# Two transformer blocks on one core: the gate columns ride on the attention's value stage, ahead of the query tiles

## What is computed

```python
hN = _rmsnorm(x, norm_g[l])
p = _split_in(hN @ w_in[l])          # m_q m_k m_v m_o m_z | m_i m_f | n_q n_kc n_vc n_ks n_vs n_kw n_vw | n_g ...
mh = _mlstm(silu(conv(p["m_q"])), silu(conv(p["m_k"])), p["m_v"],
            p["m_i"] + b_igate[l], p["m_f"] + b_fgate[l])
gates = jax.nn.sigmoid(p["n_g"] + b_nsa_gate[l])
# in _mlstm, per head: log_f = log_sigmoid(f_pre); a = cumsum(log_f)
# m_t = running maximum of (log_i - a) plus a; the decays are exp(... - m_t)
```

## Time and profile before

| what | value |
|---|---|
| median of 3 runs | 1860.36 us |
| the profiled execution's own time | 1859.45 us |
| its span | 1857.5 us |
| TensorE busy | 1838.0 us (99%) |
| VectorE busy | 1036.8 us (56%) |
| ScalarE busy | 738.3 us (40%) |
| chain that ended last | TensorE 91%, VectorE 5% |
| mean DMA rate | 118 GB/s |

### The profile page before, as it was taken

How to read it: one execution, slowest core, us unless ns; L and a number is a source line. 1 busy time by engine, 2 the same in 40 slices (tenths; PEclk the granted TensorE clock), 3 DMA queues, 4 the chain that set the end, 5 groups by cost and what they waited for, 6 DMA issues and landing times.

```text
span 1857.5 us, 25669 instructions
## 1 busy us (share of the span) xinstructions
PE 1838.0 (99%) x9436; PEld 1524.5 (82%) x9436; DVE 1036.8 (56%) x1511; ACT 738.3 (40%) x1312; POOL 219.6 (12%) x278
## 2 busy tenths in 40 slices
PE   8999999999999999999999999999999999999998
PEld 6888878777888888888889888888888888888887
DVE  7888756765576653333435797556334763333332
ACT  5345444565333542322224763335222442222332
POOL 1101041000010400000011155053000100000010
PEclk9999999999999999999999999999999999999999
DMA  8867823211476333333334433313334333332331
GB/s 312 301 177 214 227 80 92 68 37 50 131 242 206 96 91 90 102 93 94 95 93 122 140 96 95 87 29 86 102 96 152 91 91 96 96 102 88 107 94 52
DMA packets 352230, 218.86 MB, mean 118 GB/s; under 512 B 41981, under 2 KB 336202, under 8 KB 351502
## 3 DMA queue, kind: packets, MB, share of 16 engines
q1 hardware_dynamic: 340022, 173.22, 32.9%
q0 software_dynamic: 11504, 40.79, 6.6%
q10 hardware_dynamic: 616, 3.67, 0.5%
HBM read 208.83 MB, written 9.99 MB: 118 GB/s over the span
## 4 chain that ended last, share of the span: by engine, by line
PE 91%; DVE 5%; issue 2%; ACT 1%; DMA 1%; DVEq 0%; ACTq 0%; SPq 0%; POOLq 0%
PE psum L443 27%; PE psum L445 26%; PE psum L444 26%; PE psum L1674 2%; DVE ada_sum L2503 1%; DVE mlstm_qk_T L2503 1%; PE psum L1472 1%; PE psum L1502 1%; PE psum L1379 1%; PE psum L1363 1%; PE psum L1483 1%; DMA ada_w<-in_ada_w 1%; PE psum L1567 0%; DVE delta_qkv_T L2503 0%; DVE act_lo L2503 0%
## 5 line engine op out<-in xcount | busy, mean ns | idle before, releaser
L443 PE MATMUL psum<-act_hi,w_hi 128*128 128x512 f32 (+1 forms) x1632 | 651.0, 399 | 3.1 <-DVE w_lo L402 1.2
L445 PE MATMUL psum<-act_hi,w_lo 128*128 128x512 f32 (+1 forms) x1632 | 633.5, 388 | 0.0
L444 PE MATMUL psum<-act_lo,w_hi 128*128 128x512 f32 (+1 forms) x1632 | 632.9, 388 | 0.0
L402 DVE TENSOR_TENSOR w_lo<-w_raw,w_hi 128x1024 fp32r<-128x1024 f32 x304 | 382.1, 1260 | 293.5 <-ACT w_hi L394 270.9
L394 ACT ACTIVATE w_hi<-w_raw 128x1024 fp32r<-128x1024 f32 x304 | 317.6, 1052 | 179.8 <-PE psum L445 166.5
L443 PEld LDWEIGHTS psum<-act_hi,w_hi 128*128 128x128 f32 x1632 | 306.9, 188 | 69.1 <-issue 6.1
L445 PEld LDWEIGHTS psum<-act_hi,w_lo 128*128 128x128 f32 x1632 | 306.7, 188 | 64.2
L444 PEld LDWEIGHTS psum<-act_lo,w_hi 128*128 128x128 f32 x1632 | 307.2, 188 | 59.7 <-issue 1.4
L443 PE MATMUL psum<-ffn_hi,w_hi 128*128 128x512 f32 (+1 forms) x396 | 145.8, 368 | 0.0
L445 PE MATMUL psum<-ffn_hi,w_lo 128*128 128x512 f32 (+1 forms) x396 | 144.8, 366 | 0.0
L444 PE MATMUL psum<-ffn_lo,w_hi 128*128 128x512 f32 (+1 forms) x396 | 144.8, 366 | 0.0
(11 more groups left out here) (409 smaller groups left out, 2280.5 us busy)
## 6 DMA issues: line engine op xcount, KB each, us to landing
w_raw<-in_ffn_w_in SPq DMA_DIRECT2D x88, 512.0 KB, 3.7
w_raw<-in_w_in SPq DMA_DIRECT2D x68, 512.0 KB, 3.8
w_raw<-in_mix_w_in SPq DMA_DIRECT2D x52, 512.0 KB, 3.7
ada_w<-in_ada_w POOLq DMA_DIRECT2D x48, 512.0 KB, 4.9
w_raw<-in_ffn_w_out SPq DMA_DIRECT2D x32, 512.0 KB, 3.8
late_ada_w<-in_ada_w POOLq DMA_DIRECT2D x24, 512.0 KB, 4.8
w_raw<-in_ffn_w_out SPq DMA_DIRECT2D x16, 384.0 KB, 3.3
w_raw<-in_w_branch_a SPq DMA_DIRECT2D x8, 512.0 KB, 4.7
```

The lines of the kernel that those rows point to most:

```text
L402: dve.tensor_tensor(WLO[:, n % 4, :], RAW[:, n % 4, :], WHI[:, n % 4, :].bitcast(F32), ALU.subtract).then_inc(w_lo, 1)
L443: pe.matmul(out, whi, hhi, start=start, stop=False)
L444: pe.matmul(out, whi, hlo, start=False, stop=False)
L445: return pe.matmul(out, wlo, hhi, start=False, stop=stop)
```

## The change

The stage `small1` goes. `vsw1` moves ahead of `nsa1` and its rows become 288 columns wide: 256 of values, then 24 and 8 gate columns. Its weights come in three chunks of 3, 3 and 2 row blocks rather than two of four. The token groups' gate values are copied beside the values into a zeroed tile `gate_tokens`, turned by four transposes inside the first tile of `nsa1` (before its sixth row block), and `gate_rows` is written from there. All of ScalarE's gate functions now stand in tile 0 of `nsa1`; VectorE's pieces stand at k = 1, 2, 3 and 4 where they stood at 3, 4, 5 and 6, and ScalarE writes the maxima out at k = 4 and reads them back at k = 5, where it did so at 7 and after the stage. The modulation's table gives `vsw1` no blocks and `nsa1` two per tile, as before.

```diff
@@ tables
-            ("small1", 1, lambda i: ["small1"], 1),
+            ("vsw1", 1, lambda i: ["vsw0", "vsw1", "vsw2"], 5),
             ("nsa1", 1, lambda i: [(w_in, 0, 8, c, P) for c in
                                    [C_NQ + P * f for f in range(4)] + [C_KC, C_VC, C_KS, C_KW]], 8),
-            ("vsw1", 1, lambda i: ["vsw0", "vsw1"], 4),
+        VSW_KTS, VSW_COLS = ((0, 3), (3, 3), (6, 2)), 2 * P + SUB
-        ADA = {"v1": [1, 2, 2, 2, 2, 2, 2, 2], "conv1": [2, 1, 1, 1, 1, 1, 1, 0], "small1": [0], "nsa1": [2] * 8, "vsw1": [0, 0]}
+        ADA = {"v1": [1, 2, 2, 2, 2, 2, 2, 2], "conv1": [2, 1, 1, 1, 1, 1, 1, 0], "vsw1": [0, 0, 0], "nsa1": [2] * 8}
@@ SyncE, load_chunk
-                sp.dma_start(v[:, :, 0:P], wchunk(w_in, 4 * h, 4, C_VS, P)).then_inc(sem("part_loaded"), 16)
-                sp.wait_ge(sem("part_loaded"), 16 * (3 + h))
-                sp.dma_start(v[:, :, P:256], wchunk(w_in, 4 * h, 4, C_VW, P)).then_inc(w_loaded[n % 4], 16)
+                sp.dma_start(v[:, :, 0:P], wchunk(w_in, k0, kn, C_VS, P)).then_inc(sem("part_loaded"), 16)
+                sp.dma_start(v[:, :, P + 128 + 24:VSW_COLS], wchunk(w_in, k0, kn, C_I, 8)).then_inc(sem("part_loaded"), 16)
+                sp.wait_ge(sem("part_loaded"), 32 * (h + 1))
+                sp.dma_start(v[:, :, P:P + 128 + 24], wchunk(w_in, k0, kn, C_VW, P + 24)).then_inc(w_loaded[n % 4], 16)
@@ TensorE
-            tile_stage("small1", HHI, HLO)
-            tile_stage("nsa1", HHI, HLO)
+            def value_and_gate_tokens():
+                pl = Place("vsw1", 0)
+                for c, (k0, kn) in enumerate(VSW_KTS):
+                    slot = (pl.chunk + c) % 4
+                    pe.wait_ge(w_lo, pl.chunk + c + 1)
+                    for t in range(NT):
+                        o = (pe_open(pe, pl, t) if c == 0 else PS[:, pl.bank(t), :])[:, 0:VSW_COLS]
+                        for kk in range(kn):
+                            w, tok = slice(VSW_COLS * kk, VSW_COLS * kk + VSW_COLS), slice(t * P, t * P + P)
+                            pe.matmul(o, HHI[:, k0 + kk, tok], WHI[:, slot, w], start=(k0 + kk == 0), stop=False)
+                            pe.matmul(o, HHI[:, k0 + kk, tok], WLO[:, slot, w], start=False, stop=False)
+                            mm = pe.matmul(o, HLO[:, k0 + kk, tok], WHI[:, slot, w], start=False, stop=(k0 + kk == KD - 1))
+                    mm.then_inc(chunk_done, 1)
+            def gates_turned(kk):
+                if kk == 5:
+                    pl = Place("vsw1", 0)
+                    bank = pe_open(pe, pl, NT)
+                    for t in range(1, NT):
+                        pe.wait_ge(bank_free[pl.bank(t)], (pl.tile + t) // 4 + 1)
+                    for n in range(NT):
+                        mm = pe.transpose(bank[:, n * P:n * P + P], GTOK[:, n, :], ID)
+                    mm.then_inc(sem("packed_T"), 1)
+            value_and_gate_tokens()
+            tile_stage("nsa1", HHI, HLO, ready=gates_turned)
             pe.wait_ge(sem("gates_then_log_f"), 1)
             pe.wait_ge(sem("m_row_then_um"), 2)
             for n in range(NT):
                 mm = pe.transpose(PS[:, 4, n * P:n * P + P], SM[:, n * P:n * P + P], ID)
             mm.then_inc(sem("packed_T"), 1)
-            token_stage("vsw1", (0,), 4, 256)
@@ ScalarE
+            for k in range(3):
+                split_hi(act, pl, k + AHEAD)
+            tiles_ready(act, pl, 2)
+            act.wait_ge(sem("row_zero"), 1)
+            for t in range(NT):
+                ps = PS[:, pl.bank(t), :]
+                copy(GTOK[:, t, 0:2 * SUB].rearrange("p (a c) -> p a c", c=SUB)[:, :, 0:4],
+                     ps[:, 2 * P + 24:VSW_COLS].rearrange("p (a c) -> p a c", c=4))
+                copy(GTOK[:, t, 64:88], ps[:, 2 * P:2 * P + 24])
+                tile_used(copy(VSW[:, t].rearrange("p a d -> p (a d)"), ps[:, 0:256]), pl, t)
@@ ScalarE, log_gates(k)
-                elif k == 1:
                     cnt.wait()
                     cnt.mark(act.activation(r1, r0, ACT.Abs))
                     cnt.wait()
                     cnt.mark(act.activation(r1, r1, ACT.Exp, scale=-1.0))
-                elif k == 2:
                     cnt.wait()
                     act.activation(r1, r1, ACT.Ln, bias=1.0).then_inc(sem("gates_then_log_f"), 1)
-                elif k == 7:
+                elif k == 4:
                     act.wait_ge(sem("m_row_then_um"), 1)
                     act.dma_start(m_away.rearrange("o (h t) -> (o h) t", h=MH), MROW[0:4, :]).then_inc(sem("m_then_inverse_moved"), 16)
+                elif k == 5:
+                    act.wait_ge(sem("m_then_inverse_moved"), 16)
+                    act.wait_ge(sem("m_row_then_um"), 2)
+                    act.dma_start(MALL[:].rearrange("p h t -> p (h t)"), m_away.to_broadcast([P, MH * T]))\
+                       .then_inc(sem("m_then_inverse_moved"), 16)
@@ ScalarE, the loop over nsa1
                 split_hi(act, pl, k + AHEAD)
+                if k == 0:
+                    small_rows()
                 tiles_ready(act, pl, k)
@@ VectorE, m_rows(k)
-                elif k == 3:
+                elif k == 1:
                     dve.wait_ge(sem("gates_then_log_f"), 2)
...
-                elif k == 4:
+                elif k == 2:
...
-                elif k == 5:
+                elif k == 3:
...
-                elif k == 6:
+                elif k == 4:
```

More of the change, by code:

```diff
@@ L529, in two_blocks @@
         N_MOD, N_FIRST = 9, 6
-        ADA = {"v1": [1, 2, 2, 2, 2, 2, 2, 2], "conv1": [2, 1, 1, 1, 1, 1, 1, 0], "small1": [0], "nsa1": [2] * 8, "vsw1": [0, 0]}
-        ADA0 = {"v1": 1, "conv1": 16, "small1": 32, "nsa1": 32, "vsw1": 48}
+        ADA = {"v1": [1, 2, 2, 2, 2, 2, 2, 2], "conv1": [2, 1, 1, 1, 1, 1, 1, 0], "vsw1": [0, 0, 0], "nsa1": [2] * 8}
+        ADA0 = {"v1": 1, "conv1": 16, "vsw1": 32, "nsa1": 32}
         MOD_AT = {("v1", 7): 0, ("conv1", 3): 1, ("nsa1", 1): 3, ("nsa1", 5): 4, ("last", 0): 5}
@@ L2015, in _, with small_rows @@
             conv_stage("conv1", 0)
-            pl = Place("small1", 0)
-            split_hi(act, pl, AHEAD)
-            tiles_ready(act, pl, 0)
-            act.wait_ge(sem("biases_loaded"), 16 * 18)
-            tile_used(act.activation(SMR[:], PS[:, pl.bank(0), :], ACT.Identity, bias=col(SMB)), pl, 0)
+            pl = Place("vsw1", 0)
+            for k in range(3):
[8 more added lines that the diff above has]
+                tile_used(copy(VSW[:, t].rearrange("p a d -> p (a d)"), ps[:, 0:256]), pl, t)
+            def small_rows():
+                pl = Place("vsw1", 0)
+                act.wait_ge(sem("biases_loaded"), 16 * 18)
+                act.wait_ge(sem("x_moved"), 16)
+                act.wait_ge(sem("packed_T"), 1)
+                tile_used(act.activation(SMR[:], PS[:, pl.bank(NT), :], ACT.Identity, bias=col(SMB)), pl, NT)
+                act.wait_ge(bank_free[pl.bank(NT)], (pl.tile + NT) // 4 + 1)
             def log_gates(k):
@@ L2049, in _ @@
                     mod_add(3 if k == 2 else 4, pl)
-            pl = Place("vsw1", 0)
-            split_hi(act, pl, AHEAD)
-            act.wait_ge(sem("packed_T"), 1)
+            split_hi(act, Place("oz1", 0), 2)
+            act.wait_ge(sem("packed_T"), 2)
             copy(SMT[:], PS[:, 4, :].rearrange("p (n c) -> p n c", c=P)[:, :, 0:88]).then_inc(sem("packed_cols"), 1)
-            act.wait_ge(sem("m_then_inverse_moved"), 16)
-            act.wait_ge(sem("m_row_then_um"), 2)
-            act.dma_start(MALL[:].rearrange("p h t -> p (h t)"), m_away.to_broadcast([P, MH * T])).then_inc(sem("m_then_inverse_moved"), 16)
-            split_hi(act, pl, 1 + AHEAD)
-            tiles_ready(act, pl, 1)
-            for t in range(NT):
-                tile_used(copy(VSW[:, t].rearrange("p a d -> p (a d)"), PS[:, pl.bank(t), 0:256]), pl, t)
-            for k in (2, 3):
-                split_hi(act, Place("oz1", 0), k)
+            split_hi(act, Place("oz1", 0), 3)
             def gate_tile(w):
@@ L2703, in _ @@
                     a = ada(pl, ADA[name][k], a)
+                    if name == "vsw1" and k == 0:
+                        dve.memset(GTOK[:], 0.0).then_inc(sem("row_zero"), 1)
                     if name == "nsa1":
```

33 lines of the change are left out of this document (13 added, 20 removed).

## The result

Five runs of the changed kernel took 1868.76 to 1870.71 us, median 1869.78, against 1860.36 before: a ratio of 1.0053 with a 95% interval of 1.0042 to 1.0064. Five more, taken later, gave 1868.67 us, ratio 1.0041 (1.0028 to 1.0055). The profiled execution took 1869.01 us with a span of 1867.2 us. It stands 9.6 us above that of before, where I had forecast 5.6: the direction was right and the size too small.

What follows compares the result with a forecast made beforehand. TensorE was taken as the bound, with VectorE's chain setting the path to the scores: +4.6 us there and +1.0 for transfers gave +5.6 on 1859.45, 1865.05, forecast as a median of 1866.0 us, range 1861.0 to 1869.5.

Steps and rivals of the forecast that it cites:

- What TensorE saves: small1, vsw1 and four more transposes on TensorE: ideal gain 3.9 us if nothing else waits.
- the formula: Per-column matmul cost in vsw1: 288 columns cost 0.135 us, 96 matmuls 13.0 us instead of 11.7.
- The bank waits: Start of vsw1: banks 2 and 3 freed only by VectorE's last conv1 taps, 2.8 + 2.8 = 5.6 us new waiting.
- The clock: Rival, chance 0.10: array clock falls in the bank waits, slowing later vsw1 chunks; 2.4 to 4.9 us more, 1869.0 us.
- The copies at the end: End of vsw1: six copies instead of one hold the bank for nsa1's tile 0; 1.4 us (0.8 to 1.9).
- The packed chain: ScalarE's gate functions in nsa1's tile 0 delay VectorE's sums; scores of t = 2 start at 232.4, +4.6 us.
- The transfers: Beside nsa1, earlier maxima copy and residual relays delay the last modulation blocks: 1.0 us taken, up to 3.8.
- that VectorE's chain does not bind: Rival, chance 0.22: TensorE's own path decides the start of the t = 2 scores; +1.2 to +2.2 us, 1861.6 to 1862.6.
- The other side: Rival, chance 0.08: conv1 taps come 5.6 us earlier relative to TensorE, sums keep up; -3.9 us, at most -4.4.

Runs made afterwards that it cites:

- the dealt blocks: Changed kernel with four of the sixteen modulation blocks beside nsa1 dealt to vsw1 (1, 1, 2), none beside the last two tiles: 1864.46 us, ratio 1.0017.

## Why the prediction was right or wrong

**What TensorE saves.** Right. The 288-column matmuls stand 0.13 us apart, as the formula had it. With the new waits taken out the gain appears: 2.9 us of 3.9 in the interval. The missing us is the low part's wait of 0.95 at 153.89 us, which I had counted as gone with `small1` and which that kernel has again.

**The bank waits.** Right in mechanism and size: 9.21 us forecast from the stage's start to its fourth group, 9.13 measured. The second wait is 1.46 us and not 2.8 mainly because the group before it ran slowly; where that group ran at full speed, with the maxima read back late, the wait is 2.53.

**The clock.** The step that failed. I held this rival at 0.10 because 1850 to 1854 us had survived idle time at 1.00. The fall happened in all five profiled executions that had the bank waits, and in neither that had them filled. And it did not need both waits: in three of the five (the changed kernel, its repetition, the dealt blocks) the clock was already at the lower level at the third group's first matmul, behind the first wait of 2.6 us; in one it fell inside that group, in one in the second wait. Its price was 1.3 to 2.7 us against my 2.4 to 4.9: the third group's slow matmuls are hidden in the fourth's bank wait, and the second chunk is slow only in part. The row of 1850 to 1854 was the wrong precedent: it shows one stretch of gaps, and the fall to 0.54 just behind it was in the same rows. The Trainium skill ("TensorE: Matmul & The Clock Gate", Why this matters for your kernels), which I had cited and put aside, warns of gaps between bursts; here the trace agrees, with 0.53 at 154 to 158 us.

**The copies at the end.** Nearly right: 1.06 us for my 1.4.

**The packed chain.** Right, with one term too large: the wait for a low part at tile 6 is 0.6 us (204.35 us on TensorE's timeline) for my 1.0, VectorE works from 185.06 us with a single stop, and from the masked maxima to the scores it is 12.03 us for 12.1. Leaving that stop out, the stretch from `nsa1` to the masked maxima is 53.0 us in both executions (55.63 - 2.63, 56.31 - 3.31), for 52.95.

**The transfers.** Right in kind and mis-sized, the other term that failed: 1.0 us taken between 0 and 3.8, 2.6 and 3.3 measured (2.1 with the waits filled). I put it near the lower end on the thought that the weights yield, for which I had no row. The bound from volume and rate, 3.8 us, was the nearer number. Of the transfers that moved the late read-back took away a part of the wait; what makes the rest stays open.

Put together: 4.6 - 0.3 (banks and copies shorter) + 2.1 (clock) + 3.0 (blocks) = 9.4 us, against 8.2 and 10.3 in the two intervals, and 9.4 and 8.1 in the medians. With each execution's own clock and block terms (1.3 and 2.6, 2.7 and 3.3) the sum gives 8.2 and 10.3 us, the two intervals as measured. So of the 3.8 us by which the forecast of 5.6 fell short, 2.1 are the clock, 2.0 the transfers, less the 0.3. **Rivals:** that VectorE's chain does not bind, 0.22, fell with the dealt blocks: taking work off it gave 4.2 us. The other side, 0.08, would have needed bank 3 before 151.1 us; it came free near 158.

## What to carry to other kernels

When a token stage that opens all its banks at once is moved right behind a stage whose reader lags, it waits for the last reader's banks in its first microseconds; put work that needs only the oldest bank between them. An idle stretch on the engine that sums beside the main work has to be given its share of the blocks, or they pile up behind the next stage and set the path. A single row of the trace that shows a clock surviving idle time is weak evidence: here one wait of 2.6 us was enough in three executions of five, so give the fall a high chance and put its price into the sum.

## What was not expected of the hardware

One wait of TensorE, 2.6 us behind steady work at a granted 1.00, was enough in three of five executions for the clock to stand near 0.5 at the next matmul (154.20 us; 0.61 us long, where one behind a wait took 0.40 at full clock); in the other two it fell 1 to 3 us later, by the end of the second wait. It came back at different points: 2.8 us after the fourth group's start (158.19 to 160.99) in one execution of the changed kernel and 6.2 us after it (158.51 to 164.66) in another, read where the matmuls' distance goes from 0.24 back to 0.13 us. Matmuls that nobody needs, put in the waits, kept it at 1.00. And with a 1024 KB read-back onto all partitions moved out of their way, VectorE waited 1.5 us for 512 KB loads on another queue where it had waited 2.1 to 3.3: single executions, 0.6 to 1.8 us.
